# Router logits from the raw residual, norm weights at the gather, and fused bias and maxima in a three-layer kernel

## The reference, cut to what matters

```python
xl = xl + g1 * yl                                    # residual after the mixer
h = rmsnorm(xl, norm2_g) * (1 + sc2) + sh2           # what experts and router see
probs = softmax(h @ router, over 16 experts)         # 512 x 16
gates, idx = top_k(probs per expert, 64)             # each expert takes 64 tokens
xs = h[idx]; y = (silu(xs @ w1) * (xs @ w3)) @ w2 * gates
xl = xl + g2 * scatter_add(y, idx)

s = q @ k.T * 64 ** -0.5 - slope[head] * dist        # three branches: selected, window, compressed
p = softmax(s, masked); o = sum over branches of gate * (p @ v)
```

## Time and profile before

| what | value |
|---|---|
| runs | 2569.11 us median of 3 (2568.65 to 2574.59) |
| profiled execution | 2572.05 us, span 2570.6 us |
| TensorE busy | 2359.6 us, 92% of the span |
| VectorE busy | 932.6 us, 36% |
| ScalarE busy | 465.3 us, 18% |
| mean granted TensorE clock | 0.961 |

### The profile page before, as it was taken

How to read it: one execution, slowest core, us unless ns; L and a number is a source line. 1 busy time by engine, 2 the same in 40 slices (tenths; PEclk the granted TensorE clock), 3 DMA queues, 4 the chain that set the end, 5 groups by cost and what they waited for, 6 DMA issues and landing times.

```text
span 2570.6 us, 30093 instructions
## 1 busy us (share of the span) xinstructions
PE 2359.6 (92%) x12802; PEld 1150.1 (45%) x12802; DVE 932.6 (36%) x1599; ACT 465.3 (18%) x803; POOL 0.2 (0%) x4
## 2 busy tenths in 40 slices
PE   6899989699999998988799999989999888998698
PEld 1344445344444433433444444426884447544443
DVE  4537554401211113662211111125752436223661
ACT  1347200210000002021100100021112221122500
POOL 0000000000000000000000000000000000000000
PEclk9799999899999999999899999989999899998799
DMA  8134411689999993523899999941222220123052
GB/s 286 61 136 172 172 66 50 254 362 421 421 421 421 421 419 131 220 74 142 352 421 421 421 421 421 421 199 64 84 82 61 62 62 16 51 95 115 1 168 78
DMA packets 97009, 556.97 MB, mean 217 GB/s; under 512 B 13577, under 2 KB 14089, under 8 KB 40363
## 3 DMA queue, kind: packets, MB, share of 16 engines
q1 hardware_dynamic: 90432, 538.77, 53.5%
q10 hardware_dynamic: 6444, 16.28, 1.7%
HBM read 544.52 MB, written 10.49 MB: 216 GB/s over the span
## 4 chain that ended last, share of the span: by engine, by line
PE 80%; DVE 12%; ACT 3%; DMA 3%; issue 2%; ACTq 0%; SPq 0%; DVEq 0%
PE bank L214 78%; DMA fast_w<-in_w_in 2%; PE bank L217 2%; DVE residual L1381 1%; DVE scores L2731 1%; DVE wring L1289 0%; DVE squares L1347 0%; DVE max L1288 0%; ACT squares L1341 0%; DVE fast_s L1728 0%; DVE fast_s L1725 0%; DVE fast_s L1727 0%; DVE fast_s L1726 0%; DVE cf_y L1573 0%; ACT scores L2763 0%
## 5 line engine op out<-in xcount | busy, mean ns | idle before, releaser
L214 PE MATMUL bank<-normed,wring 128*128 128x512 f32 (+2 forms) x1488 | 631.1, 609 | 4.9 <-ACT normed L1546 2.1
L214 PE MATMUL bank<-experts,wring 128*64 128x512 f32 x1792 | 393.1, 593 | 1.5 <-ACT wring L1323 1.5
L214 PEld LDWEIGHTS bank<-normed,wring 128*128 128x128 f32 (+2 forms) x1488 | 248.3, 184 | 317.3 <-issue 307.8
L1347 DVE TENSOR_TENSOR squares<-squares,bank 128x512 f32<-128x512 f32 x32 | 22.0, 688 | 648.2 <-ACT squares L1341 648.2
L214 PEld LDWEIGHTS bank<-experts,wring 128*64 128x64 f32 x1792 | 127.2, 137 | 250.9 <-issue 249.1
L214 PE MATMUL bank<-experts,hs_t 128*64 128x512 f32 x896 | 212.8, 602 | 1.5 <-ACT hs_t L1362 1.5
L214 PE MATMUL bank<-give_t,y 128*128 128x512 f32 x256 | 128.6, 621 | 10.3 <-DVE residual L1381 5.9
L214 PE MATMUL bank<-pick,h_tm 128*128 128x128 f32 x1024 | 124.1, 282 | 2.4 <-DVE pick L1301 2.4
L214 PEld LDWEIGHTS bank<-experts,hs_t 128*64 128x64 f32 x896 | 68.1, 139 | 125.9 <-issue 122.5
L1381 DVE SCALAR_TENSOR_TENSOR residual<-bank,mods,residual 128x512 f32<-128x512 f32 x128 | 96.1, 751 | 73.3 <-PE bank L214 67.6
L214 PEld LDWEIGHTS bank<-pick,h_tm 128*128 128x128 f32 x1024 | 121.4, 198 | 2.6 <-issue 2.6
(11 more groups left out here) (498 smaller groups left out, 2308.3 us busy)
## 6 DMA issues: line engine op xcount, KB each, us to landing
experts<-in_exp_w SPq DMA_DIRECT2D x336, 1024.0 KB, 19.4
normed<-in_exp_w SPq DMA_DIRECT2D x48, 1024.0 KB, 19.1
wring<-in_w_in SPq DMA_DIRECT2D x52, 512.0 KB, 3.9
residual<-in_w_mod SPq DMA_DIRECT2D x24, 1024.0 KB, 5.8
cf_wmod<-in_w_mod SPq DMA_DIRECT2D x16, 1024.0 KB, 5.8
fast_w<-in_w_in SPq DMA_DIRECT2D x30, 512.0 KB, 4.4
wring<-in_cf_w SPq DMA_DIRECT2D x24, 512.0 KB, 3.6
wmod<-in_w_mod SPq DMA_DIRECT2D x8, 1024.0 KB, 10.8
```

Of the source, the lines that this page charges most:

```text
L214: return self.nc.tensor.matmul(out, lhsT, rhs, start=start, stop=stop, skip_group_check=True)
L1347: k.vec(v.tensor_tensor(m.hs[:, e, :], m.hs[:, e, :], k.bank[3 - 2 * e][:, :], ALU.mult), f"{m.name}.hs{i}.{e}")
```

## The change

1. *Logits beside the projection.* The router weights times the norm gain form a 32-column stationary for each feature block (16 columns logits, a further one of ones for the squares). It is multiplied with the raw residual block, and another with the squares, both into bank 2, behind each block of the projection. The shift's part is one vector of 16, added by a product with ones. `router_vector` makes these weights.
2. *Token roots at the turn.* The sums (logits and mean squares) are copied as one 128x144 piece and turned once; the root is then taken of 128x4 numbers and multiplied into the logits.
3. *Norm weights at the gather.* Tokens are turned from the raw X; `ht` takes the root's inverse as its scale; gain and shift go in when the gathered pieces are copied, in four activations of 128 columns per half.
4. *First expert loads early.* Layer 0: router and five units before block 3 of the out projection's weights. Layer 1: router, six units before, seven units between the second projection's blocks; `wmod` moves to the start of the stage's memory so that its slots are the ring's. Nothing waits for the last turn of H any more.
5. *Attention.* Queries are scaled by -1/(8 slope); bias and extremum are one fused instruction with an accumulator output (before: six biases, then three reductions over both heads, for which the exponentials waited); narrow weightings of both heads are joined; both heads mix into one bank and leave by one product.

```diff
 def out_sync(k, m, experts):
     for i in range(KD):
+        if i == 3:
+            p.wait_ge(*k.at("cc3.mm"))
+            router_sync(k, experts)
+            p.wait_ge(*k.at(f"hy1.product{NT - 1}"))
+            for n in range(NEARLIER):
+                unit_sync(k, experts, n)
...
 def out_tensor(k, m, experts):
-            strips_tensor(k, "e0.n", i - 1, KD, k.H[:, i - 1, :], 3)
+            route_sums_tensor(k, experts, i - 1, k.H[:, i - 1, :])
 def out_vector(k, m, experts):
     v = k.nc.vector
+    router_vector(k, experts)
     v.wait_ge(*k.at("x.again"))
+def experts_sync(k, m, first):
+    for n in range(first, len(m.order)):
         if n >= NRING:
-            p.wait_ge(*k.at(m.used(n - NRING)))
-        elif n >= NRING - 2:
-            p.wait_ge(*k.at(f"{m.name}.h_tm{NT - 1}.1"))
+            k.nc.sync.wait_ge(*k.at(m.used(n - NRING)))
+        unit_sync(k, m, n)
+def router_vector(k, m):
+    v = k.nc.vector
+    gain_vector(k, 2, "norm2_g", 8 * m.layer, m.layer, 32)
+    k.vec(v.memset(m.rg[:, :, :], 0.0))
+    k.vec(v.memset(m.rg[:, KD, NE:32], 1.0))
+    v.wait_ge(*k.at(f"{m.name}.router"))
+    shift = k.MOD[:, m.layer, 24:24 + KD, 0].unsqueeze(2).broadcast_to([P, KD, NE])
+    k.vec(v.tensor_tensor(m.rg[:, 0:KD, 0:NE], m.rt[:, :, :], shift, ALU.mult))
+    k.vec(v.tensor_reduce(m.sh[:, :], m.rg[:, 0:KD, 0:NE].rearrange("p k e -> p e k"), AXX, ALU.add))
+    k.vec(v.tensor_tensor(m.rg[:, 0:KD, 0:NE], m.rt[:, :, :], k.GA[:, 2, :].unsqueeze(2).broadcast_to([P, KD, NE]), ALU.mult),
+          f"{m.name}.gains")
+def route_sums_tensor(k, m, c, squares):
+    t, b = k.nc.tensor, k.bank[2]
+    t.wait_ge(*k.at(f"{m.name}.n.sq{c}"))
+    if c == 0:
+        t.wait_ge(*k.at(f"{m.name}.gains"))
+    for left, src in ((m.rg[:, c, :], k.X[:, c, :]), (m.rg[:, KD, :], squares)):
+        for g in range(4):
+            ins = k.mm(b[32 * g:32 * g + 32, 0:P], left, src[:, g * P:(g + 1) * P], c == 0 and src is not squares,
+                       c == KD - 1 and src is squares)
+    if c == 0:
+        ins = k.mm(b[:, P:P + NE], k.con("ones"), m.sh[:, :], False, True)
+    ins.then_inc(*k.up("tensor", f"{m.name}.n.sum{c}"))
 def route_tensor(k, m):
-    spread_tensor(k, f"{name}.n", 2)
...
+    t.wait_ge(*k.at(f"{name}.raw"))
+    k.turn(bank[1][:, 0:P], m.raw[:, 0:P]).then_inc(*k.up("tensor", f"{name}.columns"))
 def tokens_tensor(k, m, n):
-            ins = k.turn(..., k.H[:, 4 * h + c, n * P:(n + 1) * P])
+            ins = k.turn(..., k.X[:, 4 * h + c, n * P:(n + 1) * P])
 def route_scalar(k, m):
-    strips_scalar(k, f"{name}.n")
...
+    s.wait_ge(*k.at(f"{name}.mean"))
+    k.act(s.activation(m.rs[:, :], m.rs[:, :], ACT.Sqrt), f"{name}.root")
     k.act(s.activation(k.SM[:, 62:63], k.con("ones", 0, 1), ACT.Exp))
     s.wait_ge(*k.at(f"{name}.centred"))
     k.act(s.activation(m.pb[:, :, :], m.pb[:, :, :], ACT.Exp), f"{name}.exp")
-            k.act(s.copy(m.ht[...], bank[...]), ...)
+            k.act(s.activation(m.ht[...], bank[...], ACT.Identity, scale=m.rs[:, n:n + 1]), ...)
 def route_vector(k, m):
-    gain_vector(...); strips_vector(...); modulated_vector(...)
-    k.vec(v.tensor_copy(m.pet[:, :], bank[0][0:NE, :]), f"{name}.rows")
+    v.wait_ge(*k.at(f"{name}.n.sum{KD - 1}"))
+    k.vec(v.tensor_copy(m.raw[:, :], bank[2][:, 0:P + NE]), f"{name}.raw")
     v.wait_ge(*k.at(f"{name}.columns"))
-    k.vec(v.tensor_reduce(SM[:, 0:NT], lg, AXX, ALU.max))
-    k.vec(v.tensor_tensor(pr, lg, SM..., ALU.subtract), f"{name}.centred")
+    k.vec(v.tensor_scalar(m.rs[:, :], lg[:, :, NE], 1.0 / D, EPS, ALU.mult, ALU.add), f"{name}.mean")
+    v.wait_ge(*k.at(f"{name}.root"))
+    k.vec(v.reciprocal(m.rs[:, :], m.rs[:, :]))
+    k.vec(v.tensor_tensor(pr, lg[:, :, 0:NE], m.rs..., ALU.mult))
+    k.vec(v.tensor_tensor(pr, pr, m.raw[:, P:P + NE]..., ALU.add))
+    k.vec(v.tensor_reduce(SM[:, 0:NT], pr, AXX, ALU.max))
+    k.vec(v.tensor_tensor(pr, pr, SM..., ALU.subtract), f"{name}.centred")
 def gather_scalar(k, m, i, h):
-    k.act(k.nc.scalar.copy(m.xs[:, 4 * h:4 * h + 4, :], fm3(k.bank[6 + h][:, :], 4)), ...)
+    for c in range(4 * h, 4 * h + 4):
+        k.act(k.nc.scalar.activation(m.xs[:, c, :], k.bank[6 + h][:, (c % 4) * P:(c % 4 + 1) * P], ACT.Identity,
+                                     bias=k.MOD[:, m.layer, 24 + c, 0:1], scale=k.GA[:, 2, c:c + 1]), ...)
 def mixer1_sync(k, m, experts):
-    all_steps(blocks)
+    router_sync(k, experts)
+    k.nc.sync.wait_ge(*k.at(f"ad.row{NEARLY + 7}"))
+    for n in range(2, 8):
+        unit_sync(k, experts, n)
+    for n in (8, 9, 10, 11, 12, 0):
+        next(blocks)
+        k.nc.sync.wait_ge(*k.at(f"ad.row{NEARLY + n if n else len(ROWS) - 1}"))
+        unit_sync(k, experts, n)
+    unit_sync(k, experts, 1)
 def mixer1_vector(k, m, experts):
         if i == 0:
             mods_vector(k, 5)
+            router_vector(k, experts)
 def keys_vector(k, m):
-        k.vec(v.tensor_scalar(PJ[:, NQ + c, :], PJ[:, NQ + c, :], HD ** -0.5, None, ALU.mult))
+        for e, r in enumerate(HALVES):
+            k.vec(v.tensor_scalar(PJ[r, NQ + c, :], PJ[r, NQ + c, :], -HD ** -0.5 / SLOPES[2 * c + e], None, ALU.mult))
 def biased_vector(k, m, n):
+            k.vec(v.tensor_tensor_reduce(out=dst, in0=ps, in1=far, scale=slope, scalar=3e38, op0=ALU.add, op1=ALU.min,
+                                         accum_out=ms[:, b:b + 1]), f"at{n}.biased{e}.{b}")
 def weights_vector(k, m, n):
+        if hi - lo <= P:
+            k.vec(v.tensor_tensor(x, x, tot[:, :, b:b + 1].broadcast_to([P, 2, hi - lo]), ALU.mult), ...)
+        else:
+            for e in range(2):
+                k.vec(v.tensor_scalar(x, x, m.ms[:, u + e, 3 + b:4 + b], None, ALU.mult))
 def out_heads_vector(k, m, n):
+    k.vec(v.tensor_tensor(m.ys[:, 6 + hp, cols], k.bank[4][:, 0:P], m.pj[:, NZ + hp, cols], ALU.mult), f"at{n}.out")
 def exponentials_scalar(k, m, n):
+    for e in range(2):
+        for b, (lo, hi) in enumerate(spans_of(c)):
+            s.wait_ge(*k.at(f"at{n}.biased{e}.{b}"))
+            k.act(s.activation(x, x, ACT.Exp, scale=-1.0, bias=m.ms[:, u + e, b:b + 1], accum_out=...), ...)
```

More of the change, by code:

```diff
@@ L987, in out_half_tensor, with out_tensor @@
     return ins
-def out_tensor(k, m):
+def out_tensor(k, m, experts):
     t = k.nc.tensor
@@ L1131, in mixer0_vector @@
         hyena_out_vector(k, m, 1, c)
-    out_vector(k, m)
+    out_vector(k, m, experts)
     v.wait_ge(*k.at("consts.more"))
@@ L1165, in mixer0_scalar @@
     fence(k, "layer0", "scalar")
+NEARLIER = 5
 class Experts:
@@ L1188, in __init__ @@
         self.yy = at.sb("y" + L, [P, D])
+        top = Place(k.nc, (k.nc.sbuf_usable_end - 2560) // 32 * 32)
+        assert at.next <= top.next
+        self.rt = top.sb("router" + L, [P, KD, NE])
+        self.rg = top.sb("router_gain" + L, [P, KD + 1, 32])
+        self.sh = top.sb("router_shift" + L, [P, NE])
+        self.raw = top.sb("raw" + L, [P, P + NE])
+        self.rs = top.sb("roots" + L, [P, NT])
         self.xs = k.W[:, 1, :, :]
@@ L1217, in route_tensor @@
 def route_tensor(k, m):
     t, bank, name = k.nc.tensor, k.bank, m.name
-    spread_tensor(k, f"{name}.n", 2)
[L1220 to L1226, removed]
-        ins = k.turn(bank[1][:, n * NE:(n + 1) * NE], m.pet[:, n * P:(n + 1) * P], NE)
@@ L1322, in gather_scalar @@
     k.nc.scalar.wait_ge(*k.at(f"{m.name}.gather{i}.{h}"))
-    k.act(k.nc.scalar.copy(m.xs[:, 4 * h:4 * h + 4, :], fm3(k.bank[6 + h][:, :], 4)), f"{m.name}.xs{i}.{h}")
+    for c in range(4 * h, 4 * h + 4):
+        k.act(k.nc.scalar.activation(m.xs[:, c, :], k.bank[6 + h][:, (c % 4) * P:(c % 4 + 1) * P], ACT.Identity,
+                                     bias=k.MOD[:, m.layer, 24 + c, 0:1], scale=k.GA[:, 2, c:c + 1]),
+              f"{m.name}.xs{i}.{h}" if c % 4 == 3 else None)
 def up_tensor(k, m, i, e):
@@ L1551, in mixer1_scalar, with mixer1_vector @@
     fence(k, "layer1", "scalar")
-def mixer1_vector(k, m):
+def mixer1_vector(k, m, experts):
     v, bank, u, gs = k.nc.vector, k.bank, m.u, m.gs
@@ L2758, in exponentials_scalar @@
     c, hp, u = UNITS[n]
-    for b, (lo, hi) in enumerate(spans_of(c)):
-        s.wait_ge(*k.at(f"at{n}.max{b}"))
-        for e in range(2):
+    for e in range(2):
+        for b, (lo, hi) in enumerate(spans_of(c)):
             x = m.sc[:, u + e, lo:hi]
-            k.act(s.activation(x, x, ACT.Exp, bias=m.ms[:, u + e, b:b + 1], accum_out=m.ms[:, u + e, 3 + b:4 + b]),
+            s.wait_ge(*k.at(f"at{n}.biased{e}.{b}"))
+            k.act(s.activation(x, x, ACT.Exp, scale=-1.0, bias=m.ms[:, u + e, b:b + 1], accum_out=m.ms[:, u + e, 3 + b:4 + b]),
                   f"at{n}.exp" if e and b == 2 else None)
```

102 lines of the change are left out of this document (45 added, 57 removed).

## The result

The changed kernel takes 2530.59 us, median of 4 runs (2529.16 to 2530.83), beside 2571.39 for the kernel before (4 runs): ratio 0.9847, 95% interval 0.9832 to 0.9862. Measured again later it took 2532.26 (6 runs, 2528.18 to 2541.56), ratio 0.9868 (0.9848 to 0.9888). So it is 38 to 41 us faster, where 25 were forecast: right direction, outside the range.

The account below looks back on a forecast made before the run. TensorE was taken as the bound, except where stages fall into strings of small steps. Two layers at 9.65 us (14.6 - 3.6 - 1.35) and attention's 5.7 gave 25.0 less: 2569.1 to 2544 us, range 2536 to 2555.

Parts of the forecast that it names:

- Routing string: From the last column sums to the softmax sum: 17.8 us become 3.2, a gain of 14.6 us a layer.
- Sums beside the projection: Out projection: doubled sum instructions add 0.43 us to each of eight blocks, 3.6 us a layer with the ones product.
- The rival with dear sums: Sums at 0.6 us a block and a second pass in attention's fused operation: 2550.5 us, chance 0.2.
- Gather pieces, 1.35: Gather: four activations for one copy cost 1.35 us a layer, on the first pair's second half only; other pairs hidden.
- Router arithmetic, query scaling, early loads: VectorE's router steps, attention's query scaling and the earlier expert loads: each forecast to change nothing in the time.
- the ring is full again: Expert loads: remaining ten units take 25 us and land before the first release, so early loads gain nothing.
- Attention, 5.7: Attention: ring links 3.0, first two links 2.0 and lead-in 0.7, together 5.7 us less.
- the ring's 0.6 a link: Attention's cycle from output to output: one output product fewer and joined weightings save 0.6 us in each of five links.
- the lead-in 0.7 from the joined 128-column weightings: Attention ahead of its first output: 0.7 us gained by joined weightings.
- the higher clock holds in attention: Rival: the last two turns and mixings run at 2.4 GHz, 4 to 5 us more gain, 2539.5 us, chance 0.15.
- softmax sum in 3 to 3.5: Sign of being right, routing: the softmax sum comes 3 to 3.5 us behind the last sums.
- The period of 7.85: Sign of being right, out projection: 16 sum instructions take 0.86 us in a block period of 7.85 us.

Follow-up runs that it names:

- the late form: Changed kernel with the first expert units of both layers again asked for behind the stage before, router matrices still early: 2531.97 us, ratio 0.9846.
- extra products: Changed kernel plus matmuls that nothing reads, to keep TensorE busy: in attention's last two units alone 2528.19 us, ahead of the gathers too 2534.82 us.

## Why the prediction was wrong, point by point

25.0 us were forecast, 37.6 came, by the means of three executions each. Of the 12.6 over, 3.6 are a mis-sized term in the routing, 2.6 are attention, and 6.5 are the granted clock, in the routing's stretches (1.4), at the gather (0.4) and outside the edits (4.7). (The routing string gave 0.1 less than forecast.) The clock's part was in no term, and executions of one kernel differ by as much: it is mostly luck.

*Routing string, 14.6 a layer:* right. In layer 0, beside the two executions of before at the same clock (93.05 and 93.02 us), the stretch shrank by 12.7, the added sums in it are 1.8, so the string gave 14.5. The remaining execution of before (the second, 94.69) had a lower clock there; that adds 0.5 in layer 0 and 0.9 in layer 1 to the means.

*Sums beside the projection, 3.6 a layer:* the step that failed, "It can't be less, as TensorE is the bound". A busy time of 0.43 for eight is not what eight more cost; they pipeline into four strips and add 0.22, 1.8 a layer. That is 3.6 of the 12.6. There was no row for two groups back to back, and the range was closed below where a lower price was possible. The kernel before had a hint: its next product starts at 441.69, 0.36 behind the eight at 441.33. The rival with dear sums is refuted from the same row.

*Gather pieces, 1.35:* right; 1.44 and 1.49 at a like clock, and the other seven pairs hide them. The means show 1.0 and 1.3, since the gather's clock varies; that is 0.4 of the 12.6.

*Router arithmetic, query scaling, early loads:* nothing, right. The reason "the ring is full again" is right for the form with early loads, but not needed: the late form isn't full at the first release and loses nothing either.

*Attention, 5.7:* the ring's 0.6 a link is right (9.19 to 8.57). The second failed step is "the lead-in 0.7 from the joined 128-column weightings": it left out that two units' maxima stand ahead of the first output. That output came 1.9 us earlier (1.80 with the fused instruction alone, 0.35 with the joined products alone). And the fused instruction's accumulator costs 0.01, not 0.2, where 1.2 us a link had been taken off for it in the first links. Up to the fourth output 3.3 us were forecast (0.7, two links at 1.0, one at 0.6) and 6.6 came. The Trainium skill's statement weighed there (VectorE: DVE Perf Modes, section on two Vector instructions with no wait between them: an operation with an accumulator output is two instructions) agrees with the trace, 48 rows of 0.083; its zero price was the better sum. Over three executions attention gives 8.3, which is 2.6 of the 12.6, and its span among executions (69.6 to 76.2) is wider (6.6) than the whole term (5.7). All kept profiles say more: ten with the new attention code and no extra products in it took 69.2 to 76.2 us, mean 71.6, five with the old one 80.2 to 83.3, mean 82.1. They don't overlap, and the difference is 10.4, so the term was too small by more than the clock moves it.

*Not in the sum:* the granted clock outside the edits, 4.7 of the 12.6: the down projections (2.3 over both layers) and the second block (2.4). The rival "the higher clock holds in attention" named neither, and its own condition wasn't met: the last two links took 10.12 and 10.17 us at 0.71 and 0.83, where 9.25 was reached with extra products. The range took the clock of one execution as given, though the changed kernel's time moves over 13 us with it.

*What would show it:* softmax sum in 3 to 3.5, pieces, the ring's 0.6, no transfer wait: all seen. The period of 7.85 was not.

## What to carry to other kernels

Price narrow matmuls by the start-to-start distance of the next group, not by the busy time of theirs, and look at which partitions they write: into four different strips four cost about one. When a reduction is folded into another pass, count it in every place where it stands ahead of the first result, not only in the steady links. And before a stage's gain is credited to an edit, compare its granted clock and profile the same kernel twice: here a stage that no edit touches moves by 6 to 8 us between executions of one kernel (649.0 and 642.8, 641.8 and 649.4).

## What the runs showed of the hardware that was not expected

- Four 128-column float32 matmuls with 32 columns of weights take 0.24 us into four strips and 0.90 into one.
- VectorE's fused add, minimum and accumulate over 512 columns takes 692 ns beside 688 for the plain form; its accumulator row of 83 ns overlaps the main row.
- With TensorE kept busy through the routing, the 64 rows of a gather took 7.38 us and not 9.32 in one profile; in two others with the same instructions they took 8.77 to 9.01, as the clock fell just ahead of them. The granted clock isn't a function of the program alone: attention of one kernel ran at 0.83, 0.77 and 0.73 in three executions.
